# A two-block f32 network on one core: x loaded in pieces, first weight slabs in halves, attention steps laid between the latent query tiles, and the next norm's operands made from the residual stream

## What is computed

```python
def first_block(x, ...):
    h = concat([meta, x])                                  # 272 tokens
    h = h + attention_mixer(rms_norm(h, g), ...)           # layer 0
    h = h + sq_relu_mlp(rms_norm(h, g), w_up, w_down)
    h = h + short_conv_mixer(rms_norm(h, g), ...)          # layer 1
    h = h + sq_relu_mlp(rms_norm(h, g), w_up, w_down)
    return h[:, 16:]

def attention_mixer(h, ...):
    c_q, c_kv, k_pe, fq, fk, fv, f_logit = split(h @ w_in)
    q = rms_norm(c_q) @ w_uq;  kv = rms_norm(c_kv) @ w_ukv     # 8 heads of 96
    q, k = rope_tail(rms_norm(q)), rope_tail(rms_norm([k_nope, k_pe]))
    o_mla = causal_softmax_attention(q, k, v)
    o_fox = causal_softmax_attention(rms_norm(fq), rms_norm(fk), fv, cum_log_forget)
    return concat([o_mla, o_fox]) @ w_out
```

## Time and profile before

| | |
|---|---|
| median of three runs | 1374.69 us |
| profiled execution, its span | 1373.33 us, 1371.6 us |
| TensorE busy | 1322.3 us, 96% |
| VectorE, ScalarE, GpSimd busy | 71%, 54%, 33% |
| HBM read | 228.17 MB, 167 GB/s over the span |
| granted TensorE clock | 0.99 in the mean |

### The profile page before, as it was taken

One profiled execution on the slowest core, in us unless ns is written; L12 is line 12 of the kernel. 1 busy time (PEld: TensorE's weight loads), 2 busy tenths in 40 slices (PEclk: granted clock), 3 DMA queues, 4 the chain that ended last, 5 costly groups with the idle time before them and its releaser, 6 DMA issues. The chain is left out here.

```text
span 1371.6 us, 29146 instructions
## 1 busy us (share of the span) xinstructions
PE 1322.3 (96%) x10774; PEld 1288.3 (94%) x10774; DVE 969.3 (71%) x1440; ACT 735.5 (54%) x1204; POOL 445.8 (33%) x462
## 2 busy tenths in 40 slices
PE   5999999999999999999999999999999899999996
PEld 5787699999999999999989999999999889999996
DVE  6767567664578677655655569998569798999844
ACT  5454655444444444444455547665445785766642
POOL 3532044321111433311545423333125534343300
PEclk9998999999999999999999999999999999999998
DMA  7440044555545555555534555554554446555451
GB/s 268 166 141 32 1 152 159 184 185 183 184 181 189 180 184 184 185 184 183 205 134 155 185 185 185 183 183 145 201 207 154 154 162 208 185 184 183 147 198 54
DMA packets 34507, 230.52 MB, mean 168 GB/s; under 512 B 3838, under 2 KB 4990, under 8 KB 10662
## 3 DMA queue, kind: packets, MB, share of 16 engines
q1 hardware_dynamic: 33652, 226.47, 47.4%
q10 hardware_dynamic: 770, 2.90, 0.6%
HBM read 228.17 MB, written 1.05 MB: 167 GB/s over the span
## 5 line engine op out<-in xcount | busy, mean ns | idle before, releaser
L365 DVE TENSOR_TENSOR wlo<-raw,whi 128x1024 fp32r<-128x1024 f32 (+1 forms) x448 | 548.2, 1229 | 92.1 <-ACT whi L360 91.0
L400 PE MATMUL ps<-xhi,whi 128*128 128x256 f32 (+2 forms) x2064 | 585.0, 283 | 21.2 <-DVE wlo L365 17.8
L401 PE MATMUL ps<-xlo,whi 128*128 128x256 f32 (+2 forms) x2064 | 583.2, 283 | 0.0
L402 PE MATMUL ps<-xhi,wlo 128*128 128x256 f32 (+2 forms) x2064 | 581.9, 282 | 0.0
L360 ACT ACTIVATE whi<-raw 128x1024 fp32r<-128x1024 f32 (+1 forms) x448 | 448.9, 1009 | 134.1 <-PE ps L402 130.0
L400 PEld LDWEIGHTS ps<-xhi,whi 128*128 128x128 f32 x2064 | 390.2, 189 | 26.5 <-issue 20.8
L402 PEld LDWEIGHTS ps<-xhi,wlo 128*128 128x128 f32 x2064 | 390.9, 189 | 0.0
L401 PEld LDWEIGHTS ps<-xlo,whi 128*128 128x128 f32 x2064 | 388.5, 188 | 0.3
L400 PE MATMUL ps<-hhi,whi 128*128 128x256 f32 (+1 forms) x1184 | 335.2, 283 | 3.3 <-issue 2.6
L402 PE MATMUL ps<-hhi,wlo 128*128 128x256 f32 (+1 forms) x1184 | 334.4, 282 | 0.0
L401 PE MATMUL ps<-hlo,whi 128*128 128x256 f32 (+1 forms) x1184 | 334.2, 282 | 0.0
(11 more groups left out here) (261 smaller groups left out, 1293.2 us busy)
## 6 DMA issues: line engine op xcount, KB each, us to landing
raw<-w SPq DMA_DIRECT2D x184, 1024.0 KB, 4.8
raw<-w SPq DMA_DIRECT2D x40, 768.0 KB, 4.2
h<-x_fm ACTq DMA_DIRECT2D x1, 1088.0 KB, 6.3
out_fm<-h SPq DMA_DIRECT2D x8, 128.0 KB, 2.0
ws<-ws_src ACTq DMA_DIRECT2D x1, 512.0 KB, 4.6
bs<-bs_rows ACTq DMA_DIRECT2D x1, 512.0 KB, 5.4
consts<-constants ACTq DMA_DIRECT2D x1, 508.0 KB, 9.6
q_fox<-decay_rows SPq DMA_DIRECT2D x1, 340.0 KB
```

The costliest lines, as they stand in the source:

```text
L365: nc.vector.tensor_tensor(wlo[:, j % HLR, 0:n], raw[:, slot, col:col + n], whi[:, j % HLR, 0:n].bitcast(F32), ALU.subtract).then_inc(wlo_d ...
L400: nc.tensor.matmul(o, hi, xh, start=start, stop=False)
L401: nc.tensor.matmul(o, hi, xl, start=False, stop=False)
L402: mm = nc.tensor.matmul(o, lo, xh, start=False, stop=stop)
```

## The change

Seven edits. (1) h is loaded in four pieces, the first two slabs in parts; consts and most of params come after the slabs. TensorE runs 46 matmuls on a zeroed tile first. Xhi of the first norm is written directly as h x gain, even tiles by VectorE, odd ones by ScalarE, and xlo by VectorE; `first_units` does the hi products of units 0 and 1 before their wlo products. The sum of squares moves to GpSimd, its statistic behind unit 4. (2) The fox q units come before the shared one; the fox spreads, `fox_normed`, v's turns and forget-gate steps lie one or two units later. (3) The query tiles use banks 2 to 5; scores 0 to 3 and turns 0 and 1 lie between them. `q_stats` is cut into three parts, in turns 2 to 4; its values are copied out of PSUM before the root. (4) Key pairs are finished in steps 4, 5, 6 and 8. (5) The second halo item comes after head 8, and its copy is made for head 8 ahead. (6) Splits for attn_out are put into steps 11, 13, 15. (7) In every residual phase ScalarE writes xhi = h x gain from h, and VectorE xlo = h x gain - xhi, after the coming unit's wlo; GpSimd's xlo and VectorE's gain go. ScalarE's residual loops are written out.

```diff
+        def act_gained(act, n, kt, c0, t):
+            nc.scalar.activation(xhi[:, kt, c0:c0 + t], h[:, kt, c0:c0 + t], ACT.Identity,
+                                 scale=par(NORM_GAIN[n], kt)).then_inc(xhi_done, 1)
+        def dve_xlo(dve, n, kt, c0, t):
+            dve.wait_ge(xhi_done, kt + (8 * n + 1))
+            nc.vector.scalar_tensor_tensor(out=xlo[:, kt, c0:c0 + t], in0=h[:, kt, c0:c0 + t],
+                                           scalar=par(NORM_GAIN[n], kt), in1=xhi[:, kt, c0:c0 + t].bitcast(F32),
+                                           op0=ALU.mult, op1=ALU.subtract).then_inc(xlo_done, 1)
...
+                        ahead(dve, split_lo, p, it, j, last)
                         if n != 8:
-                            dve.wait_ge(tile_free, kt + (p.tile0 + 1))
-                            dve_gain(dve, n, kt, jt % 2, c0, t)
-                        ahead(dve, split_lo, p, it, j, last)
+                            dve_xlo(dve, n, kt, c0, t)
...
                         act.wait_ge(tile_free, kt + (p.tile0 + 1))
                         if n != 8:
-                            act_xhi(act, n, kt, jt % 2, c0, t)
+                            act_gained(act, n, kt, c0, t)
...
-                    if n != 8:
-                        pool_xlo(pool, n, kt, jt % 2, c0, t)
                     pool_ssum(pool, n, kt, jt % 2, c0, t)
...
+        items = ([("d", 0)] + [("h", i) for i in range(HEADS)] + [("h", HEADS), ("d", 1)]
+                 + [("h", HEADS + i) for i in range(1, HEADS)])
         NIT = len(items)
+        LATE = {11: U_Q + 1, 13: U_Q + 2, 15: U_Q + 3}
+        KEY_SPREAD = {5: 1, 6: 2, 7: 3}
+        KEY_FINAL = {4: 0, 5: 1, 6: 2, 8: 3}
...
+                    half = UB * P
+                    sp.dma_start(raw[:, 0, 0:half], src[0][:, 0:half]).then_inc(s("unit0_loaded"), 16)
+                    sp.wait_ge(x_loaded[1], 16)
+                    sp.dma_start(raw[:, 0, half:cols], src[0][:, half:cols]).then_inc(raw_full[0], 16)
+                    for i in (0, 2, 3):
+                        sp.wait_ge(x_loaded[i], 16)
+                    sp.dma_start(raw[:, 1, 0:half], src[1][:, 0:half]).then_inc(s("unit2_loaded"), 16)
+                    sp.dma_start(raw[:, 1, half:cols], src[1][:, half:cols]).then_inc(raw_full[1], 16)
+                    sp.dma_start(raw[:, 2, 0:cols], src[2]).then_inc(raw_full[2], 16)
+                    sp.dma_start(consts[:, :], consts_in).then_inc(consts_in_done, 16)
+                    sp.dma_start(raw[:, 3, 0:cols], src[3]).then_inc(raw_full[3], 16)
...
-            pe.wait_ge(consts_in_done, 16)
+            pe.wait_ge(s("warm_set"), 1)
+            for _ in range(WARM):
+                nc.tensor.matmul(ps[:, 7, 0:SEQ], chi[:, 0, 0:P], chi[:, 0, 0:SEQ], start=True, stop=True)
...
+            def first_units():
+                o = [ps[:, take(), 0:T0] for _ in range(2)]
+                for u in range(2):
+                    pe.wait_ge(whi_done, u + 1)
+                    for b in range(8):
...
+                        nc.tensor.matmul(o[u], whi[:, u, b * P:(b + 1) * P], xhi[:, b, :], start=b == 0, stop=False)
+                    for b in range(8):
...
+                        nc.tensor.matmul(o[u], whi[:, u, b * P:(b + 1) * P], xlo[:, b, :], start=False, stop=False)
+                for u in range(2):
+                    pe.wait_ge(wlo_done, u + 1)
+                    for b in range(8):
+                        mm = nc.tensor.matmul(o[u], wlo[:, u, b * P:(b + 1) * P], xhi[:, b, :], start=False,
+                                              stop=b == 7)
+                    mm.then_inc(unit_done, 1)
...
+            for x in range(HEADS):
+                query_tile(x)
+                if x == 3:
+                    turn_v(0, (0, 1, 2))
+                if 2 <= x <= 4:
+                    scores(x - 2)
+                if x == 5:
+                    turn(0)
+                if x == 6:
+                    scores(3)
+            turn(1)
+            key_spread(0)
+            for st in range(4, NIT + 3):
                 if st < NIT:
                     scores(st)
...
+                if st in KEY_SPREAD:
+                    key_spread(KEY_SPREAD[st])
+                if st < NIT + 2:
                     turn(st - 2)
...
+                if j in (2, 3, 4):
+                    q_stats(j - 2)
...
+            act.wait_ge(s("warm_set"), 1)
+            nc.scalar.activation(four[:, 0:1], chi[:, 0, 0:1].bitcast(F32), ACT.Sqrt).then_inc(s("sqrt_ready"), 1)
...
+            for i in range(2):
+                first_xhi(2 * i)
+                first_xlo(2 * i)
+                first_xlo(2 * i + 1)
+            first_xhi(4)
+            first_xhi(6)
+            for kt in range(4, KT):
+                first_xlo(kt)
+            for j in range(LA):
                 split_lo(dve, 0, j, 8)
...
+                if st == 6:
+                    roots(3)
...
+                pool.wait_ge(sq_done, kt + 1)
+                pool.wait_ge(ssum_done, kt + 1)
+                nc.gpsimd.tensor_tensor(ssum[:, :], ssum[:, :], first_sq[kt], ALU.add).then_inc(ssum_done, 1)
```

More of the change, by code:

```diff
@@ L48 @@
 LA = 3
+WARM = 46
 PHASES = [
@@ L920, in turn_v, with q_stats @@
-            def turn_v(w):
+            def q_stats(k):
+                if k == 0:
+                    pe.wait_ge(q_eps_step, 6)
+                m = META if k == 2 else P
+                for x in range(-1, 6):
+                    if k == 0 and x >= 0:
+                        pe.wait_ge(n_sq[3], x + 1)
+                    tile = q_eps if x < 0 else q_sq[:, x, :]
+                    if k == 2:
+                        lhs = q_sq_d[:, META * (x + 1):META * (x + 2)]
+                    else:
+                        lhs = tile[:, NQ + k * P:NQ + (k + 1) * P]
+                    if x < 0:
+                        rhs = consts[:, K_LATENT:K_LATENT + HEADS]
+                    elif Q_KIND[x] == "nope":
+                        rhs = pair_cols(Q_AT[x])
+                    else:
+                        rhs = consts[:, K_QUAD + HEADS * Q_AT[x]:K_QUAD + HEADS * (Q_AT[x] + 1)]
+                    mm = nc.tensor.matmul(ps[0:m, 6, 2 * P + k * HEADS:2 * P + (k + 1) * HEADS], lhs, rhs, start=x < 0,
+                                          stop=x == 5)
+                if k == 2:
+                    mm.then_inc(n_ss, 1)
@@ L922, in turn_v @@
+            def turn_v(w, which):
                 freed, n = tile_left((TL_V if w == 0 else TL_FV) + 3)
                 pe.wait_ge(freed, n)
-                for a, n in KEYS:
-                    bank = take_ring()
+                for kt in which:
+                    a, n = KEYS[kt]
+                    if w:
+                        bank = take_ring()
+                    else:
+                        bank = 6 + kt % 2
+                        pe.wait_ge(n_root, 3)
+                        pe.wait_ge(vt_done, 4 if kt == 2 else 3)
@@ L963, in _, with query_tile @@
                     k_stats()
-            pe.wait_ge(c_lo, 5)
-            for x in range(HEADS):
-                bank = take()
+            def query_tile(x):
+                if x == 0:
+                    pe.wait_ge(c_lo, 5)
+                if x in (2, 3):
+                    pe.wait_ge(vt_done, 5 - x)
+                if x < 2 or x >= 4:
+                    freed, n = tile_left(TL_Q + x - 4)
+                    pe.wait_ge(freed, n)
+                bank = tile_bank(TL_Q + x)
                 o = ps[:, bank, 0:T0]
@@ L1374, in low, with step @@
                                         chi[rows, t, C1:T0].bitcast(F32), ALU.subtract).then_inc(olo_done, 1)
-            for st in range(NIT + 4):
+            def step(st):
                 if st < NIT:
@@ L1385, in _ @@
+            for st in range(4, NIT + 4):
+                if st in LATE:
+                    to(LATE[st])
+                step(st)
+            dve.wait_ge(s("params_loaded"), 16)
             for _ in dve_log_sigmoid(dve, par("lam", 0, NB), log_lam[:, :], tmp[:, 0, 0:NB], tmp[:, 1, 0:NB],
@@ L1556, in to @@
                     rnd = done[0] // UB + (j + LA) // UB
-                    split_hi(act, rnd, (j + LA) % UB, 8, first=rnd == 0)
+                    split_hi(act, rnd, (j + LA) % UB, 1 if done[0] + LA == p.units - 1 else 8, first=rnd == 0)
                     done[0] += 1
@@ new lines, in high, with step @@
+            def high(i):
+                w, hd = heads[i][3:5]
+                rows = HALF[hd % 2]
+                act.wait_ge(pv_done, i + 1)
+                nc.scalar.activation(chi[rows, 4 * (1 - w) + hd // 2, C1:T0], ps[rows, 4 + i % 2, 0:T1],
+                                     ACT.Copy).then_inc(ohi_done, 1)
+            def step(st):
+                if st < NIT:
+                    exps(st)
+                if 2 <= st < NIT + 2:
+                    turned(st - 2)
+                if st == 6:
+                    roots(3)
+                if st >= 3 and items[st - 3][0] == "h":
+                    high(items[st - 3][1])
```

(18 more changed lines are left out.)

494 lines of the change are left out of this document (265 added, 229 removed).

## The result

The changed kernel takes 1364.79 us in the median of five (1361.61 to 1372.0), against 1374.69 before: a ratio of 0.9932, 95% interval 0.9914 to 0.995. That is 9.9 us less, half of the 19.8 that I forecast; the time is inside the range, at its upper end. The profiled execution took 1372.0 us over a span of 1370.3, the slowest of the five.

What follows compares the result with a forecast made beforehand. TensorE, busy 96%, was taken as the bound, its weight matmuls unchanged. Savings 9.0 + 2.6 + 4.9 + 1.1 + 2.2 = 19.8 us took 1373.33 to 1353.5; with 1.36 for the median, 1354.9 us, range 1348 to 1366.

Steps and rivals of the forecast that it cites:

- The start: First units: x in pieces, half slabs and warming let unit 2 start at 14.5 instead of 24.22; 9.0 us taken.
- rival B: Start bound by landings: pieces share full engines, slab halves wait for x; 5 us won, not 9; 1358.9; chance 0.09.
- First phase: Waits of 1.8 us for the head inverse and 1.0 for v's copy get one more unit of cover; 2.6 us.
- Attention: Query tiles and attention: 4.9 us from head steps between tiles, 1.1 from waits for v_tok and the halo item.
- The term for the clock: Start of attention: 13.2 us at half clock cost 6.4 us, which cutting and spreading the statistics would save.
- The term of 1.1 us for waits: Latent queries and attention: waits of 0.7 us for v_tok and 1.2 at a halo item shrink; ends 0 and 1.9.
- I count 1.5 us of new waits: Query tiles with head steps: VectorE at 2.5 to 2.9 us a tile against TensorE's 2.2; deducted from 6.4.
- Rival A: Attention: the clock falls all the same, in a statistics third or a fill wait; costs 6.4 us; 1361.3; chance 0.13.
- D: Rival: low clock holds through attention from scores 1 on, 3.26 us a head; slower, 1394; chance 0.03.
- Rival C: Attention step 6: table switch with a drain, 2.7 us more on ScalarE; 1357.6; chance 0.05.
- Norms: Seven residual-to-norm places: 1.2 us before the last up stage, 1.0 at the other six; 2.2 us together.
- rival E: Waits move: VectorE late by 0.5 us or more each step until keys are done, 8 us lost; 1362.9; chance 0.06.

Runs made afterwards that it cites:

- e8: The changed kernel without the 46 warming matmuls on the zeroed tile; 1365.26 us.
- e6: The changed kernel with the two pads and remaining parameters issued two weight-slab rounds later; 1364.09 us.
- e5: The changed kernel with query tiles and attention back in the order of the kernel before; 1365.07 us.
- e12: The changed kernel with the second halo item ahead of head 8, pads and parameters two slab rounds later, ScalarE's held-back copies a whole step earlier; 1358.0 us.
- e14: The kernel of e12 a second time, beside e13; 1356.78 us.
- e13: The changed kernel, halo item still behind head 8, with pads and parameters two slab rounds later and ScalarE's held-back copies a whole step earlier; 1362.76 us.
- e1: The changed kernel with the second halo item back ahead of head 8, last key pair in step 7, query scale in step 8; 1363.88 us.
- e7: The kernel before with the norm edit alone; 1372.92 us against 1374.26.
- e11: The changed kernel with query tiles and attention in the order of before, and pads and parameters two slab rounds later; 1362.03 us.
- e9: e1 with ScalarE's held-back copies meant to come earlier; the edit left the queue unchanged, so it is e1's program again; 1363.07 us.
- e10: e9 (the same program as e1) with pads and parameters two slab rounds later; 1361.78 us.
- e2: The changed kernel with the first two statistics thirds moved back between the last query tiles; 1370.96 us.
- e3: The changed kernel with each statistics third cut to one matmul, leaving out most of the statistic; 1363.26 us.
- e4: The changed kernel with scores and turns taken out from between the query tiles; 1367.44 us.

## Why half of the forecast gain did not come

**The start.** Taken 9.0, measured 8.05. The warming was over at 8.3, as I had it (8.5). The terms that were off are landings. The second piece of x was there at 6.80 us, where I had 4.8; ScalarE stood in front of it for 1.5 us, so that its copy of whi 0 began at 7.22, not 6.2, with its slab half already there. The other halves are issued only when pieces of x have landed: TensorE waited 0.6 us for whi 1, and unit 2's half let ScalarE begin at 13.38, where I had the copy done by 11.1. Then wlo 2 is the last thing waited for, at 16.17 instead of 14.5. That is rival B's mechanism, with a quarter of its price of 4 us. VectorE's third wlo took 1.65 us, not 1.23, and made 0.4 of it: it started 0.2 us behind a pair of GpSimd's additions. In e8 it started 0.3 us ahead of them and took 1.24.

```profile
6.80 0.52 ACT L1667 ACTIVATE xhi<-h,params 128x272 fp32r<-128x272 f32 x1 [1.51 <-DMA h<-x_fm]
...
7.22 1.05 ACT L1672 ACTIVATE whi<-raw 128x1024 fp32r<-128x1024 f32 x1
...
13.38 1.06 ACT L1678 ACTIVATE whi<-raw 128x1024 fp32r<-128x1024 f32 x1 [1.12 <-DMA raw<-w]
...
25.99 1.06 ACT L361 ACTIVATE whi<-raw 128x1024 fp32r<-128x1024 f32 x1 [3.62 <-DMA raw<-w]
```

**First phase.** Taken 2.6, measured 0.2 in the profiled execution (the key tiles are 8.28 us earlier, the start 8.05). It isn't as little in every execution: in the nine profiles in which the inverse came in time, the first query tile starts 9.0 to 9.8 us earlier than before, which leaves 1.0 to 1.7 for the first phase beside a start of 8.05. The step that failed is the share of 0.53 in a steady stretch that "leaves room": this is no steady stretch. All that was moved behind the first slabs lands between 16 and 36 us, where the DMA share is 0.98 in the changed kernel, 0.67 before and 0.74 in e6. The last row above shows what follows: a copy waits 3.62 us for its slab, and ScalarE and VectorE are late for the inverse. I had argued the cover in matmuls of TensorE, three microseconds of them, and never asked whether the engines that make the inverse would be on time.

**Attention.** Taken 4.9 and 1.1, measured nothing in the median (e5) and 5.5 in the profiles of e12 and e14. The term for the clock was right in kind: with no fall TensorE's busy time drops from 75.08 to 69.75 us. That is 5.3 us, where I had 6.4: the clock was 0.91 over 77.44 us, some 13.9 us' worth at half clock, and each cost some 0.38 us rather than 0.5. The term of 1.1 us for waits is 0.2 even there, 2.4 us idle before and 2.2 in e12. Why nothing was left in the changed kernel is seen best in e8, which has its attention and no fall at the statistics:

```profile
87.75:164.87 77.12, 71.68 (x474) 52.98 (x473) 50.90 (x158) 46.33 (x154) 6.98 (x11) 0.98 0.08 28
```

TensorE is busy 3.4 us less than before and idle 3.1 us more. What failed is "the halo item moves behind head 8 and its copy is done early": head 8's values waited 2.0 us for that copy (2.4 in e13), and the fall behind that wait cost time again. And "I count 1.5 us of new waits" looked for them in the query tiles, while they came in the later steps: 0.8 us in the changed kernel, 1.2 in e6 and 2.9 in e1, from the three subtractions that I had mentioned as put off and then costed at nothing. A copy and a subtraction of 2.3 us, one behind the other, in a step of 3.26 whose maxima take their place behind it: the rows for that sum were all there.

**Rival A, the clock.** It holds in part. In the profiled execution it fell in the statistics, for some 20 us, and once more behind the 2.0 us wait. Over all profiles cutting the statistics into thirds did what it was meant to, though not always: with the 45 in one block (the kernel before, e5, e7, e11) the clock fell at them in four of four, for 7 to 14 us; with the thirds in turns 2 to 4 and the fill (the changed kernel, e1, e6, e8, e9, e10, e12, e13, e14) in two of nine, the changed kernel and e10. But it isn't what separates the medians: the mean granted clock is 0.992 over the changed kernel's five runs and 0.991 over 23 runs of the kernel before. My argument against A, a wait of 1.8 us that left the clock at 1.00, doesn't hold: e7 has the same wait in the same order of work, and the clock fell behind it. D did not come: the longest fall ended after some 20 us.

**Rival C.** The two switches are there (1.28 us at 123.08, the root's activation at 124.38), again with no drain. The Trainium skill (ScalarE: Activation LUTs, What ACT_TABLE_LOAD costs) has 2.66 us per switch; the trace shows 1.30.

**Norms.** Taken 2.2, measured 1.3 (e7). The wait of 1.42 is gone in the changed kernel and 0.56 in e7. At the other places, for which I had 1.0 us, a step of 0.34 stays between two starts (661.57 to 661.91 before a_v) where it was 0.43: 0.1 each. The term that was mis-sized is VectorE's xlo: taken at 0.43 us, it has a median of 0.90 in the 56 of the residual phases, because in 43 of them an operation of GpSimd is at work when it starts. In e7 one tile's addition follows the last by 2.37 us, with VectorE at work all the time, where I had some 2.1 against TensorE's 2.13:

```profile
1152.86 0.41 DVE L1531 TENSOR_TENSOR h<-ps,h 128x256 f32<-128x256 f32 x1
1153.19 1.21 DVE L365 TENSOR_TENSOR wlo<-raw,whi 128x1024 fp32r<-128x1024 f32 x1
...
1154.33 0.98 DVE L481 SCALAR_TENSOR_TENSOR xlo<-h,params,xhi 128x256 fp32r<-128x256 f32 x1
1155.23 0.41 DVE L1531 TENSOR_TENSOR h<-ps,h 128x256 f32<-128x256 f32 x1
```

**The sum.** 8.05 + 0.2 + 0 + 1.3 = 9.55 us, against 9.9 measured. It mixes one slow execution with medians of others, so that it comes so close is luck; with 1.0 to 1.7 for the first phase it is 10.4 to 11.1. The 9.55 is 10.25 short of the forecast's 19.8: 6.0 in attention, 2.4 in the first phase, 0.95 at the start and 0.9 in the norms. The chance of 0.06 for rival E, waits that move (to 1362.9), was too small: it is what happened, at another place than I named.

## What to carry to other kernels

When a step is put off to a later place, cost it there as it will stand in every queue: the copy on one engine and the subtraction on the next form a chain, and put at the same step it holds up the second engine for both; a step of lead between the two took TensorE's idle time in attention from 5.15 us to 2.2 and the median from 1361.8 to 1358.0 and 1356.8. A short item in a pipeline must be looked at from its consumer: which copy does the next item need, and what stands ahead of that copy. The price of an instruction has to come from a row in which the same neighbour is at work: the xlo of 0.43 us cost 0.90 beside GpSimd's additions. And transfers that are pushed back out of the first microseconds don't vanish; read the DMA share of the stretch in which they will land, not that of a steady one.

## What the runs showed of the hardware

**A fall behind a wait in busy work.** In all seven profiles with the halo item behind head 8 (the changed kernel, e2, e3, e4, e6, e8, e13) the granted clock falls to 0.50, which is 1.2 of 2.4 GHz, right behind the wait of 2.0 to 2.4 us at that item, for some 3 to 7 us. In the five with the new order but without that wait (e1, e9, e10, e12, e14) it never falls there. Behind other waits and at the statistics it falls in one execution and not in another of the same order of work. Seven profiles wait 1.5 to 1.9 us for the head inverse: the clock falls within some 1 us behind it in e5, e7 and e9, and stays at 1.00 in the kernel before, the changed kernel, e2 and e4. The kernel before and e7 both wait 2.0 us for the norm's sum near 23 us; only e7's clock falls behind it. What decides that stays open.

**What a fall costs.** e12 ran at 1356.43 us with a mean granted clock of 0.997 and at 1366.84 with 0.987; the changed kernel at 1361.61 with 0.996 and at 1372.0 with 0.987. In both a mean lower by 0.01 goes with a time longer by some 10 to 12 us. A mean lower by 0.001 is about a microsecond, so single executions of these kernels can't be compared.

**VectorE beside GpSimd.** Of two operations that start 0.04 us apart the second takes longer and the first keeps its time: xlo 0.99 us behind an addition of 0.74, and 0.47 with an addition of 1.03 behind it (e7 and the changed kernel, above). All 56 xlo of the changed kernel's residual phases agree with it: 0.86 to 1.00 us behind a running operation of GpSimd, 0.47 or 0.48 otherwise.

**A slow lead the clock column doesn't show.** Without warming the first 24 matmuls start 0.23 us apart until 13.85, with a granted clock of 1.00 in the row:

```profile
8.00:12.00 4.00, 3.78 (x17) 3.80 (x17) 3.46 (x8) 2.18 (x5) 0.00 (x0) 1.00 0.90 266
```

In the kernel before, the same slow lead took 3.1 us, here 5.6; it isn't of fixed length.
